# Which engine issues the up matrices: from SP's queue to ScalarE's in a 32-expert loop

## The chip, the cores and the metric

One Trainium2 chip, one core. The metric is the device time of one execution in microseconds (us).

## What is computed

One step of a diffusion backbone for 128 context and 512 latent tokens of width 1024, in fp32: a modulated norm, an input projection, two groups of attention heads (retention and gated linear attention), an output projection, then a mixture of 32 experts. Only the last part touches the change. Every token picks one of 4 groups and in it 2 of 8 experts, and the picked experts are summed with their weights:

```python
def hier_moe(t, ...):
    ...
    for e in range(N_EXPERTS):
        hdn = jax.nn.silu(t @ expert_w_gate[e]) * (t @ expert_w_up[e])
        y = y + combine[:, e:e + 1] * (hdn @ expert_w_down[e]).astype(jnp.float32)
    return y.astype(t.dtype)
```

An expert has three matrices of 1 MB each: gate and up (1024 x 256) and down (256 x 1024). All 32 are used, 96 MB in all, and none of it is used twice.

## The kernel before

Each engine runs a program of its own; semaphores connect them. Up to the router the kernel streams the projection weights through four buffers and builds the attention. The last third of the time is the expert loop.

**Buffers.** There are `WEIGHTS = 7` expert buffers (`exb`, line 36 and below). Each has a gate part, an up part and a down part. The first seven experts are loaded by SP early, as the memory under their buffers comes free (lines 560 to 580). Expert `e` of 7 to 31 goes to buffer `e % 7` and can be loaded only when expert `e - 7` has been used: gate and up when its gate-up product is done (semaphore `gate_up_filled`, in the code `gu_filled`), down when its down product is done (`y_filled`).

**SP** issues the 25 x 3 loads in one order (lines 582 to 587): wait for `gu_filled`, gate (line 524), up (line 525), wait for `y_filled`, down (line 528). A load that is ready stands behind every wait ahead of it. After the last expert SP issues the loads of five blocks of rows (`x_rows`) and of the final norm's row.

**TensorE** runs, for each expert `e`: `gate_up(e + 1)` (line 1850: 32 products of 128x64 against 128x256, which wait for both matrices to land and for the turned tokens), `turn_tokens(e + 2)` (line 1841), `down(e)` (line 1866) and `turn_hidden(e + 1)` (line 1858).

**ScalarE** runs, for each expert: `silu(e + 1)` (line 992) as soon as `gate_up(e + 1)` is done, then `turned_tokens(e + 2)` (line 986), the copy of the turned tokens out of PSUM that `gate_up(e + 2)` waits for. It has a DMA queue of its own, on which it issues `hn_rows` and `x_rows` (lines 969 and 970) before the loop and nothing in the loop.

**VectorE** multiplies silu and up, copies the turned hidden rows and scales the result. **GpSimd** gathers the tokens of the expert four ahead (line 735) and scatters the result rows of each expert (line 744) by indirect DMAs on a third queue.

Of the kernel before, what the change touches and what calls it, by code (L numbers as in the profile page):

```python
# [5 lines left out]
P = 128  # L6
# [12 lines left out]
NE = 32  # L19
# [10 lines left out]
UNIT = KC * ITEM  # L30
# [5 lines left out]
WEIGHTS = 7  # L36
# [143 lines left out]
def build(nc, inp, outs):  # L180
# [10 lines left out]
    with ExitStack() as ctx:  # L191
# [3 lines left out]
        def sem(name):  # L195
            return ctx.enter_context(nc.semaphore(name))
# [116 lines left out]
        exb = [A[:, n * 3 * UNIT:(n + 1) * 3 * UNIT] for n in range(3)] + [B[:, n * 3 * UNIT:(n + 1) * 3 * UNIT] for n in range(3)]  # L313
# [47 lines left out]
        def where(job):  # L361
            n = job_at[job]
            return n % NB1, n // NB1
# [4 lines left out]
        def is_filled(eng, job):  # L368
            b, turn = where(job)
            eng.wait_ge(filled[b], turn + 1)  # L370
# [31 lines left out]
        for i in range(len(IN_ITEMS)):  # L402
            n = i - LEVEL_AFTER + 1
# [22 lines left out]
        for job, block in plan_outputs():  # L426
            n = BLOCKS_OUT.index(block) if block else None
# [28 lines left out]
        def w_src(n):  # L456

            load, slot = LOADS[n], ring[n % RING]
            if load[0] == "ada":
                _, m, i = load  # L460
                return (w_ada[0].rearrange("(p k) c -> p k c", k=KC)[:, 2 * i:2 * i + 2, m * D:(m + 1) * D],
                        slot.rearrange("p (k c) -> p k c", k=2))
            if load[0] == "rest":
                c0 = 2 * D + load[1] * ITEM
                return (w_ada[0, :, c0:c0 + ITEM].rearrange("(p k) c -> p k c", k=KC), slot.rearrange("p (k c) -> p k c", k=KC))
            if load[0] == "in":
                _, c0, w = IN_ITEMS[load[1]]
                return (w_in[0, :, c0:c0 + w].rearrange("(k p) c -> p k c", k=KC),
                        slot[:, 0:KC * w].rearrange("p (k c) -> p k c", k=KC))
            return (w_out[0, :, load[1] * ITEM:(load[1] + 1) * ITEM].rearrange("(k p) c -> p k c", k=KC),  # L470
                    slot.rearrange("p (k c) -> p k c", k=KC))

        def load_used(eng, n):

            load = LOADS[n]
            if load[0] == "ada":
                _, m, i = load
                if i < 3:
                    eng.wait_ge(ada_used, 3 * m + i + 1)
                else:  # L480
                    eng.wait_ge(filled[where(("mr",))[0]] if m == 0 else scale_summed, 1)
            elif load[0] == "rest":
                dve.wait(eng, ("acc", load[1]))
            elif load[0] == "in":
                name, _, w = IN_ITEMS[load[1]]
                is_filled(eng, ("v", load[1], CTX) if name in ("gv", "rv") else ("p", load[1], max(1, w // P) - 1, "ctx"))
            else:
                is_filled(eng, ("mix", CTX, load[1]))
# [5 lines left out]
        gu_landed = [sem(f"gate_up_weights{n}_landed") for n in range(WEIGHTS)]  # L494
# [14 lines left out]
        yo_ready, yo_written, over_read = sem("final_ready"), sem("final_written"), sem("overflow_read")  # L509
        factors_ready, factors_begun = sem("row_factors_ready"), sem("row_factors_begun")  # L510

        block = ctx.enter_context(nc.Block())


        @block.sync
        def _(sp):
# [6 lines left out]
            def load_gate_up(e, b, s):  # L523
                sp.dma_start(exb[b][:, 0:UNIT], ewg_v[bass.ds(e * P, P), :]).then_inc(s, 16)  # L524
                sp.dma_start(exb[b][:, UNIT:2 * UNIT], ewu_v[bass.ds(e * P, P), :]).then_inc(s, 16)  # L525

            def load_down(e, b, s):
                sp.dma_start(exd[b], ewd_v[bass.ds(e, 1)].rearrange("e (j p) n -> p (e j) n", p=P)).then_inc(s, 16)  # L528

            ewg_v = ewg.rearrange("a e (p k) f -> (a e p) (k f)", p=P)  # L530
            ewu_v = ewu.rearrange("a e (p k) f -> (a e p) (k f)", p=P)
            ewd_v = ewd.rearrange("a e f n -> (a e) f n")

            def mod_rows(m, dst):
                for cond in range(2):
# [25 lines left out]
            for e in range(3):  # L561
                load_gate_up(e, e, gu_landed[e])
                load_down(e, e, dn_landed[e])
# [5 lines left out]
            load_used(sp, len(LOADS) - 1)  # L569
            load_gate_up(3, 3, gu_landed[3])  # L570
            load_down(3, 3, dn_landed[3])
            dve.wait(sp, ("hn", LT - 1))
            sp.wait_ge(x2_written, 16 * LT)
            load_gate_up(4, 4, gu_landed[4])
            load_down(4, 4, dn_landed[4])
            dve.wait(sp, ("hn", CTX))
            sp.wait_ge(x2_written_ctx, 16)
# [4 lines left out]
            for e in range(WEIGHTS, NE):  # L582
                b = e % WEIGHTS
                sp.wait_ge(gu_filled, e - WEIGHTS + 1)
                load_gate_up(e, b, gu_landed[b])
                sp.wait_ge(y_filled, e - WEIGHTS + 1)
                load_down(e, b, dn_landed[b])
            sp.wait_ge(y_filled, NE - WEIGHTS + 1)
# [6 lines left out]
            with sp.If(n_over > 0):  # L595
                with sp.Fori(0, n_over) as i:
                    e = sp.value_load(over[0:1, bass.ds(i + 1, 1)], min_val=0, max_val=NE - 1)
# [183 lines left out]
        def _(sc):  # L781
# [7 lines left out]
            f = nc.scalar.activation  # L789
# [59 lines left out]
            for i, (name, _, w) in enumerate(IN_ITEMS):  # L849
# [7 lines left out]
                else:  # L857
                    for c in range(max(1, w // P)):
                        n = 2 * (i - 3) + c
                        for part, lo, hi in (("lat", 0, N_LAT), ("ctx", N_LAT, T)):  # L860
# [9 lines left out]
                            elif name in ("rq", "rk"):  # L870
                                a, h = ("rq", "rk").index(name), 2 * ((i - 3) % 2) + c
                                s = float(P) ** -0.5 if a else 1.0
# [32 lines left out]
                n = i - LEVEL_AFTER + 1  # L905
# [75 lines left out]
            def turned_tokens(e, n, free):  # L981

                sc.wait_ge(xg_turned, e + 1)
                if free is not None:
                    sc.wait_ge(gu_filled, free)
                f(xte[n], bank[n][:, :].rearrange("p (k s) -> p k s", k=KC), ACT.Copy).then_inc(xte_ready, 1)

            def silu(e, n, free):
                sc.wait_ge(gu_filled, e + 1)
                if free is not None:  # L990
                    sc.wait_ge(hid_ready, free)
                f(sil[n], bank[2 + n][:, 0:P], ACT.Silu).then_inc(sil_ready, 1)  # L992

            is_filled(sc, ("idx",))
            sc.wait_ge(none_set, 1)
            for e in range(TOKS):
# [3 lines left out]
            turned_tokens(0, 0, None)  # L1000
            dve.wait(sc, "dest")
            silu(0, 0, None)
            turned_tokens(1, 1, None)
            for e in range(NE - 1):
                silu(e + 1, (e + 1) % 2, e if e else None)
                if e + 2 < NE:
                    turned_tokens(e + 2, e % 2, e + 1)
            n_over = sc.value_load(over[0:1, 0:1], min_val=0, max_val=MAX_OVER)
# [967 lines left out]
```

## Time and profile before

| | |
|---|---|
| three runs | 832.07, 832.17, 835.92 us; median 832.17 |
| the profiled execution | 833.67 us, of which the profile's span is 831.9 us |
| TensorE busy | 725.4 us (87% of the span) |
| VectorE, ScalarE, GpSimd busy | 393.4, 155.7, 206.9 us |
| moved by DMA | 186.02 MB, mean 224 GB/s over the span |
| SP's queue | 159.94 MB, ScalarE's 12.55 MB, GpSimd's 12.83 MB |
| first gate-up product of the loop | 547.3 us from the span's start |

A busy share is of one engine. The DMA share is the mean over the core's 16 DMA engines, and can come out a little over 1 because packets overlap. A DMA-issuing instruction is no busy time of its engine: the profile shows how long the engine's sequencer stood in it. How long the data then takes to arrive is told apart, as the time to landing. Windows are counted from the span's start.

### The profile page before, as it was taken

The numbers are of one execution on the slowest core, as the hardware profiler recorded it, in microseconds if no ns is written. First come the engines' busy times: TensorE is split into PE (matmuls) and PEld (weight loads), VectorE is DVE, ScalarE is ACT, GpSimd is POOL, SyncE is SP. The second block draws the span as 40 slices with busy tenths as digits, with TensorE's granted clock in tenths as the row PEclk, the third lists the DMA queues.
The fourth block names the chain that finished last, engine by engine and source line by source line (L and its number), as shares of the span: only waits on it lengthen the run. The fifth ranks groups of instructions, "written<-read, shape, count | busy, mean of one in ns | idle before, by whom it ended". The sixth has DMA issues, their size and how long they took to land.

```text
span 831.9 us, 10844 instructions
## 1 busy us (share of the span) xinstructions
PE 725.4 (87%) x4297; PEld 467.4 (56%) x4297; DVE 393.4 (47%) x782; ACT 155.7 (19%) x257; POOL 206.9 (25%) x239
## 2 busy tenths in 40 slices
PE   3899996999999999999899999889999777788730
PEld 1655553558888565677788885455554433344310
DVE  0462399587576675656734335712233112111227
ACT  2320421011322215313101111111111001001002
POOL 1500044233333101112300000124444323323213
PEclk8989898999999999999999999999999999989975
DMA  9945304322233434335249317949999999999955
GB/s 353 369 146 155 102 1 137 117 82 94 79 102 102 131 123 137 103 118 144 71 180 404 155 51 299 369 143 368 374 380 384 397 387 389 394 390 385 386 199 240
DMA packets 74307, 186.02 MB, mean 224 GB/s; under 512 B 10012, under 2 KB 47044, under 8 KB 65296
## 3 DMA queue, kind: packets, MB, share of 16 engines
q1 hardware_dynamic: 62688, 159.94, 52.3%
q0 software_dynamic: 6144, 12.83, 4.7%
q10 hardware_dynamic: 5424, 12.55, 4.0%
q8 instruction: 35, 0.57, 0.3%
q14 instruction: 16, 0.13, 0.0%
HBM read 174.48 MB, written 17.10 MB: 230 GB/s over the span
## 4 chain that ended last, share of the span: by engine, by line
PE 61%; DMA 12%; DVE 11%; SPq 8%; issue 3%; ACT 2%; POOL 2%; DVEq 0%; POOLq 0%; ACTq 0%
PE bank L1633 18%; DMA weights_x_h<-in_expert_w_up 10%; PE bank L1850 7%; PE bank L1796 7%; PE bank L1623 4%; PE bank L1866 4%; SPq L525 3%; DVE qkv_gates_tables L1113 3%; SPq L524 3%; SPq L528 2%; DMA weights_x_h<-in_w_ada 2%; PE bank L1661 2%; PE bank L1752 2%; PE bank L1743 2%; PE bank L1695 2%
## 5 line engine op out<-in xcount | busy, mean ns | idle before, releaser
L1633 PE MATMUL bank<-weights_x_h 128*128 128x128 f32 (+3 forms) x672 | 190.7, 445 | 1.4 <-DVE weights_x_h L1079 1.4
L1633 PEld LDWEIGHTS bank<-weights_x_h 128*128 128x128 f32 (+1 forms) x672 | 103.5, 191 | 89.6 <-issue 88.2
L1850 PE MATMUL bank<-qkv_gates_tables,attention 128*64 128x256 f32 x480 | 59.4, 403 | 16.5 <-DMA qkv_gates_tables<-in_expert_w_up 15.6
L1448 DVE TENSOR_TENSOR attention<-attention,bank 128x128 f32<-128x128 f32 x32 | 9.2, 288 | 135.8 <-ACT attention L992 135.8
L1623 PE MATMUL bank<-weights_x_h 128*128 128x256 f32 x320 | 70.3, 380 | 0.0
L1623 PEld LDWEIGHTS bank<-weights_x_h 128*128 128x128 f32 x320 | 60.4, 190 | 9.3 <-DVE attention L1097 0.8
L1850 PE MATMUL bank<-weights_x_h,attention 128*64 128x256 f32 x416 | 52.2, 408 | 13.6 <-DMA weights_x_h<-in_expert_w_up 13.6
L1796 PE MATMUL bank<-weights_x_h 128*128 128x256 f32 x256 | 57.8, 388 | 0.0
L1850 PEld LDWEIGHTS bank<-qkv_gates_tables,attention 128*64 128x64 f32 x480 | 35.6, 146 | 35.9 <-DMA qkv_gates_tables<-in_expert_w_up 17.2
L635 POOL TENSOR_TENSOR small<-small 128x1 f32<-128x1 f32 (+1 forms) x20 | 15.7, 783 | 153.9 <-DVE small L1033 153.9
L1796 PEld LDWEIGHTS bank<-weights_x_h 128*128 128x128 f32 x256 | 49.6, 195 | 7.0
L1469 DVE SCALAR_TENSOR_TENSOR attention<-bank,slot_weights,qkv_gates_tables 128x512 f32<-128x512 f32 x32 | 24.0, 751 | 61.7 <-PE bank L1866 61.7
L1113 DVE SCALAR_TENSOR_TENSOR qkv_gates_tables<-weights_x_h,small,qkv_gates_tables 128x256 f32<-128x256 f32 x112 | 51.1, 536 | 0.0
L1850 PEld LDWEIGHTS bank<-weights_x_h,attention 128*64 128x64 f32 x416 | 30.8, 146 | 31.2 <-DMA weights_x_h<-in_expert_w_up 14.9
L1113 DVE SCALAR_TENSOR_TENSOR weights_x_h<-weights_x_h,small 128x256 f32<-128x256 f32 x112 | 48.0, 506 | 0.0
L992 ACT ACTIVATE attention<-bank 128x128 f32<-128x128 f32 x32 | 8.9, 278 | 203.5 <-PE bank L1850 203.4
L684 POOL TENSOR_TENSOR qkv_gates_tables<-qkv_gates_tables 128x512 f32<-128x512 f32 x8 | 15.2, 1895 | 114.4 <-ACT qkv_gates_tables L880 114.4
L744 POOL DMA_INDIRECT pick_rows<-attention,slot_rows_now x32 | 32.5, 1016 | 28.1 <-POOL slot_rows_now L741 28.1
L735 POOL DMA_INDIRECT attention<-hn_rows,slot_tokens_now x32 | 31.4, 982 | 28.0 <-POOL slot_tokens_now L730 24.6
L741 POOL COPY slot_rows_now<-slot_rows 128x1 int32<-128x1 int32 x32 | 22.6, 707 | 43.4 <-DVE attention L1469 43.4
L730 POOL COPY slot_tokens_now<-slot_tokens 64x1 int32<-64x1 int32 x32 | 5.8, 180 | 102.6 <-PE bank L1841 75.0
L1866 PE MATMUL bank<-qkv_gates_tables,attention 128*64 128x512 f32 x120 | 29.0, 604 | 0.0
(286 smaller groups left out, 997.9 us busy)
## 6 DMA issues: line engine op xcount, KB each, us to landing
weights_x_h<-in_w_ada SPq DMA_DIRECT2D x24, 1024.0 KB, 7.7
qkv_gates_tables<-in_expert_w_gate SPq DMA_DIRECT2D x15, 1024.0 KB, 19.0
qkv_gates_tables<-in_expert_w_up SPq DMA_DIRECT2D x15, 1024.0 KB, 27.2
qkv_gates_tables<-in_expert_w_down SPq DMA_DIRECT2D x15, 1024.0 KB, 26.7
weights_x_h<-in_w_in SPq DMA_DIRECT2D x14, 1024.0 KB, 7.6
weights_x_h<-in_expert_w_gate SPq DMA_DIRECT2D x13, 1024.0 KB, 20.9
weights_x_h<-in_expert_w_up SPq DMA_DIRECT2D x13, 1024.0 KB, 26.4
weights_x_h<-in_expert_w_down SPq DMA_DIRECT2D x13, 1024.0 KB, 26.6
```

Of the source, the lines that this page charges most:

```text
L524: sp.dma_start(exb[b][:, 0:UNIT], ewg_v[bass.ds(e * P, P), :]).then_inc(s, 16)
L525: sp.dma_start(exb[b][:, UNIT:2 * UNIT], ewu_v[bass.ds(e * P, P), :]).then_inc(s, 16)
L735: pool.indirect_dma_start(xg[b], None, hn_dram[:, :], bass.IndirectOffsetOnAxis(ap=idxc[b][:, :].bitcast(U32), axis=0), bounds_check=T - 1 ...
L741: nc.gpsimd.tensor_copy(sidxc[n][:, :], sidx[:, col]).then_inc(sidxc_set, 1)
L744: pool.indirect_dma_start(ys_dram[:, :], bass.IndirectOffsetOnAxis(ap=sidxc[n][:, :].bitcast(U32), axis=0), yb[n], None, bounds_check=2 * ...
L1113: ins = v.scalar_tensor_tensor(acc, w[:, k], cS[:, a, k:k + 1], acc, ALU.mult, ALU.add)
L1469: v.scalar_tensor_tensor(yb[n], bank[4 + n][:, :], weight, g2s[n], ALU.mult, ALU.mult).then_inc(y_ready, 1)
L1623: ins = mm(ps[:, 0:ITEM], hT[:, k, t * P:(t + 1) * P], wt[:, k, :], start=(k == 0), stop=(k == KC - 1))
L1633: ins = mm(ps[0:m, 0:hi - lo], wt[:, k, c * m:(c + 1) * m], hT[:, k, lo:hi], start=(k == 0), stop=(k == KC - 1))
L1796: ins = mm(ps[:, 0:ITEM], hT[:, k, t * P:(t + 1) * P], wt[:, k, :], start=(k == 0), stop=(k == KC - 1))
L1850: ins = mm(bank[2 + n][j * SLOTS:(j + 1) * SLOTS, 0:2 * P], xte[n][:, k, :], exgu[b][:, :, k, j * P:(j + 1) * P], start=(k == 0), stop=(k ...
L1866: ins = mm(bank[4 + n][half * SLOTS:(half + 1) * SLOTS, :], hidT[n][:, j, :], exd[b][:, j, half * 512:(half + 1) * 512], start=(j == 0), s ...
```

## The change

The up matrices of experts 7 to 31 are issued by ScalarE on its own queue, each behind the silu of the expert that used the buffer before. SP issues gate and down as before. The loads of experts 0 to 6 and those of the overflow loop keep their place. The three views of the weights move out of SP's block so that both can use them.

```diff
+            def load_gate(e, b, s):
+                sp.dma_start(exb[b][:, 0:UNIT], ewg_v[bass.ds(e * P, P), :]).then_inc(s, 16)
...
             for e in range(WEIGHTS, NE):
                 b = e % WEIGHTS
                 sp.wait_ge(gu_filled, e - WEIGHTS + 1)
-                load_gate_up(e, b, gu_landed[b])
+                load_gate(e, b, gu_landed[b])
                 sp.wait_ge(y_filled, e - WEIGHTS + 1)
                 load_down(e, b, dn_landed[b])
...
+            def load_up(e, b, s):
+                sc.dma_start(exb[b][:, UNIT:2 * UNIT], ewu_v[e * P:(e + 1) * P, :]).then_inc(s, 16)
...
             silu(0, 0, None)
+            load_up(WEIGHTS, 0, gu_landed[0])
             turned_tokens(1, 1, None)
             for e in range(NE - 1):
                 silu(e + 1, (e + 1) % 2, e if e else None)
+                if e + 1 + WEIGHTS < NE:
+                    load_up(e + 1 + WEIGHTS, (e + 1) % WEIGHTS, gu_landed[(e + 1) % WEIGHTS])
                 if e + 2 < NE:
                     turned_tokens(e + 2, e % 2, e + 1)
```

ScalarE in the loop, before (L992 is the silu, L986 the copy of the turned tokens; `attention` is the memory area that holds both results):

```order
L992 ACTIVATE attention<-bank3 128x128
L986 ACTIVATE attention<-bank0 128x512
L992 ACTIVATE attention<-bank2 128x128
L986 ACTIVATE attention<-bank1 128x512
L992 ACTIVATE attention<-bank3 128x128
```

and with the change, at the experts whose buffers lie in the areas `attention` and `qkv_gates_tables` (L995 is the silu, L998 the new issue, L989 the copy):

```order
L995 ACTIVATE attention<-bank2 128x128
L998 DMA attention<-in_expert_w_up 128x2048
L989 ACTIVATE attention<-bank1 128x512
L995 ACTIVATE attention<-bank3 128x128
L998 DMA qkv_gates_tables<-in_expert_w_up 128x2048
L989 ACTIVATE attention<-bank0 128x512
```

The issue stands between the silu and the copy that TensorE's next gate-up product waits for.

SP's queue from expert 7 on, before:

```order
L524 DMA qkv_gates_tables<-in_expert_w_gate 128x2048
L525 DMA qkv_gates_tables<-in_expert_w_up 128x2048
L528 DMA qkv_gates_tables<-in_expert_w_down 128x2x1024
L524 DMA qkv_gates_tables<-in_expert_w_gate 128x2048
L525 DMA qkv_gates_tables<-in_expert_w_up 128x2048
```

and with the change (L532 gate, L535 down), each with the semaphore that it waits for:

```order
L532 DMA qkv_gates_tables<-in_expert_w_gate 128x2048 [waits gate_up_filled]
L535 DMA qkv_gates_tables<-in_expert_w_down 128x2x1024 [waits expert_done]
L532 DMA qkv_gates_tables<-in_expert_w_gate 128x2048 [waits gate_up_filled]
L535 DMA qkv_gates_tables<-in_expert_w_down 128x2x1024 [waits expert_done]
L532 DMA weights_x_h<-in_expert_w_gate 128x2048 [waits gate_up_filled]
```

The up matrix has left the queue; before, it stood behind the wait for the down product (`expert_done`) of the expert before its own.

## Rows read from the trace of the kernel before

**Rows 1.** The page: the span in 40 slices, busy tenths of the DMA engines.

```profile
DMA  9945304322233434335249317949999999999955
```

**Rows 2.** Windows of the expert loop; columns as in the first line.

```profile
core 0: us, PE busy (x) PEld busy (x) DVE busy (x) ACT busy (x) POOL busy (x), PEclk, DMA share, GB/s
...
553.00:557.00 4.00, 3.95 (x34) 2.43 (x35) 0.95 (x2) 0.07 (x1) 0.62 (x1) 1.00 1.00 421
558.00:559.00 1.00, 1.00 (x8) 0.29 (x4) 0.00 (x0) 0.26 (x1) 0.28 (x1) 1.00 0.42 103
559.00:560.00 1.00, 1.00 (x9) 0.39 (x7) 0.38 (x1) 0.00 (x0) 0.68 (x1) 1.00 0.09 16
560.00:561.00 1.00, 1.00 (x12) 0.68 (x10) 1.00 (x3) 0.00 (x0) 0.46 (x1) 1.00 0.65 94
561.00:562.00 1.00, 1.00 (x12) 0.68 (x10) 0.23 (x1) 0.00 (x0) 0.27 (x1) 1.00 0.66 238
...
570.00:633.00 63.00, 63.00 (x486) 33.84 (x486) 18.95 (x40) 8.53 (x20) 28.71 (x40) 1.00 1.02 375
633.00:785.00 152.00, 119.81 (x837) 62.58 (x835) 32.23 (x68) 14.87 (x34) 47.16 (x65) 0.92 1.02 391
```

**Rows 3.** Timeline of SP's queue: start us, us, engine line op out<-in.

```profile
550.96 0.33 SPq L524 DMA_DIRECT2D qkv_gates_tables<-in_expert_w_gate  x1
...
559.53 0.38 SPq L528 DMA_DIRECT2D qkv_gates_tables<-in_expert_w_down  x1
...
561.29 0.94 SPq L525 DMA_DIRECT2D qkv_gates_tables<-in_expert_w_up  x1
...
600.30 7.87 SPq L525 DMA_DIRECT2D qkv_gates_tables<-in_expert_w_up  x1
```

**Rows 4.** Timeline of TensorE and ScalarE at experts 0 to 2.

```profile
552.30 0.28 ACT L992 ACTIVATE attention<-bank 128x128 f32<-128x128 f32 x1
...
553.31 3.67 PE L1850 MATMUL bank<-qkv_gates_tables,attention 128*64 128x256 f32 x32
...
557.03 0.28 ACT L992 ACTIVATE attention<-bank 128x128 f32<-128x128 f32 x1 [3.97 <-PE bank L1850]
...
557.66 0.60 ACT L986 ACTIVATE attention<-bank 128x512 f32<-128x512 f32 x1 [0.35 <-PE bank L1841]
...
559.68 3.67 PE L1850 MATMUL bank<-qkv_gates_tables,attention 128*64 128x256 f32 x32
```

**Rows 5.** Timeline of TensorE: gate-up products of experts 15 and 31.

```profile
644.27 3.67 PE L1850 MATMUL bank<-qkv_gates_tables,attention 128*64 128x256 f32 x32 [1.67 <-DMA qkv_gates_tables<-in_expert_w_up]
...
789.59 3.67 PE L1850 MATMUL bank<-weights_x_h,attention 128*64 128x256 f32 x32 [1.30 <-DMA weights_x_h<-in_expert_w_up]
```

**Rows 6.** Line 525 on SP's queue: ns min/median/max, first and last start us.

```profile
L525 SPq DMA_DIRECT2D qkv_gates_tables<-in_expert_w_up x15: 432/2613/7865, 432.0 to 752.8; - x15
```

**Rows 7.** Timeline of ScalarE's and SP's queues near 442 us.

```profile
441.80 0.33 ACTq L969 DMA_DIRECT2D hn_rows<-attention  x1
442.17 0.45 ACTq L970 DMA_DIRECT2D x_rows<-weights_x_h  x1
...
441.31 1.24 SPq L566 DMA_DIRECT2D onorm<-mod_rows  x1
442.58 4.08 SPq L566 DMA_DIRECT2D onorm<-mod_rows  x1
```

**Rows 8.** DMA issues: out<-in, queue, count, KB each, median us to landing.

```profile
hn_rows<-attention ACTq DMA_DIRECT2D x5, 512.0 KB, 6.8
...
onorm<-mod_rows SPq DMA_DIRECT2D x4, 128.0 KB, 21.9
```

**Rows 9.** Windows before the loop, columns as in rows 2.

```profile
515.00:520.00 5.00, 5.00 (x13) 2.15 (x12) 4.38 (x27) 0.00 (x0) 0.00 (x0) 1.00 1.00 411
440.00:445.00 5.00, 5.00 (x25) 4.41 (x24) 2.44 (x3) 0.00 (x0) 0.00 (x0) 1.00 1.04 398
445.00:450.00 5.00, 4.36 (x25) 3.66 (x23) 1.87 (x3) 1.04 (x2) 0.00 (x0) 1.00 0.97 375
```

More of the change, by code:

```diff
@@ L510, in build @@
         factors_ready, factors_begun = sem("row_factors_ready"), sem("row_factors_begun")
+        ewg_v = ewg.rearrange("a e (p k) f -> (a e p) (k f)", p=P)
+        ewu_v = ewu.rearrange("a e (p k) f -> (a e p) (k f)", p=P)
+        ewd_v = ewd.rearrange("a e f n -> (a e) f n")
         block = ctx.enter_context(nc.Block())
@@ L525, in load_gate_up @@
                 sp.dma_start(exb[b][:, UNIT:2 * UNIT], ewu_v[bass.ds(e * P, P), :]).then_inc(s, 16)
+            def load_gate(e, b, s):
+                sp.dma_start(exb[b][:, 0:UNIT], ewg_v[bass.ds(e * P, P), :]).then_inc(s, 16)
             def load_down(e, b, s):
                 sp.dma_start(exd[b], ewd_v[bass.ds(e, 1)].rearrange("e (j p) n -> p (e j) n", p=P)).then_inc(s, 16)
-            ewg_v = ewg.rearrange("a e (p k) f -> (a e p) (k f)", p=P)
-            ewu_v = ewu.rearrange("a e (p k) f -> (a e p) (k f)", p=P)
-            ewd_v = ewd.rearrange("a e f n -> (a e) f n")
             def mod_rows(m, dst):
```

## The prediction

> **What bounds the kernel now.** I read three views, in this order. First the page's row of DMA activity [rows 1]: from the slice that begins near 562 us to the one that ends near 790 us the sixteen DMA engines stand at 9 tenths or more, which they do nowhere else for long. So the expert loop is where the change can matter, and the transfers are the first suspect. Second the windows of that stretch [rows 2]: the DMA share is 1.02 from 570 to 785 us, at 375 and then 391 GB/s, so no engine has idle time there; only between 558 and 562 us is there a hole, with shares of 0.42, 0.09, 0.65 and 0.66. Third, TensorE's own rows. While it still lives on the seven buffered experts it starts a gate-up product every 559.68 - 553.31 = 6.37 us [rows 4]; later it starts one every (789.59 - 644.27) / 16 = 9.08 us and waits each time for an up matrix to land [rows 5]. 9.08 is more than 6.37, so from about expert 15 the transfers alone set the pace, and they have been behind since 562 us. What SP does follows from that: its issues, 0.33 us when nothing is queued, grow to 2.61 us in the median and 7.87 us at most [rows 3, 6], because the queue in front of it is full. That time on SP looks like a bound and is none: the engines behind it are at 1.02 all the while.
>
> **The change, part by part.** Transfers, bytes and destinations stay the same; 25 up matrices (experts 7 to 31) change issuer and place in the order.
>
> *Removed from SP:* 25 issues, 2.61 us each in the median [rows 6], some 65 us of SP's time. They cost nothing now and give nothing back: while SP stands in them, the engines are full [rows 2]. The cover is the backlog of matrices that are issued and not yet moved; if it were gone, an issue would be back at 0.33 us anyway. The Trainium skill says the same in general (DMA: Bandwidth & Descriptors, section Issuing engines are not separate DMA queues): starting transfers from several engines saves only the time of initiating them, since all run on the same engines. By that rule alone the change would give 832.2, the upper end of the forecast's own range below; the rows go beyond it in one place, the hole, because an issue there is late and not long.
>
> *The hole, the one gain.* SP waits in order: gate and up of expert 7 at 550.96 us, then a wait until `down(0)` is done, at 559.53, for down 7, then gate 8, and up 8 only at 561.29 [rows 3]. But the buffer of up 8 is free when the gate-up product of expert 1 ends, and ScalarE knows this: its silu of expert 1 runs from 557.03 to 557.31 [rows 4]. With the change up 8 is issued at 557.31, 4 us earlier than now and 2.2 us before anything else. Gate 7 shows how long an issue takes to reach the engines: issued at 550.96, they are full by 553 [rows 2, 3], so up to 2.0 us. Up 8 then runs from about 559, for 1.05 MB / 421 GB/s = 2.5 us, until down 7 and gate 8 arrive after 561.5 as now. It fills the idle shares of 559 to 562: 0.91 + 0.35 + 0.34 = 1.60 us of all engines. Below that the gain could be 0, if the engine that ends last was not one of the idle ones; above it 2.18 us, the whole hole from 558 on. I take 1.6, since a share of 0.09 means that nearly every engine stood still. All that follows is transfer-bound, so a head start of 1.6 us stays a head start until the last gate lands.
>
> *Up 7* is now issued behind the first silu, whose end is 552.30 + 0.28 = 552.58 [rows 4], about 1.3 us later than its present place right behind gate 7. Gate 7 occupies the engines until about 553 + 2.5 = 555.5, so up 7 still finds them busy: nothing.
>
> *Added to ScalarE:* 25 issues at 0.33 to 0.45 us [rows 7], 11 us in all, between a silu and the copy of the next but one expert's turned tokens. That copy now starts at 557.66, 0.35 us behind the silu's end, and ends at 558.26; TensorE needs it at 559.68 [rows 4], 1.42 us later. An issue of 0.45 us moves it by 0.1 us: nothing. Behind the copy nothing is queued on ScalarE but the next silu, which waits for the next gate-up product.
>
> *Order of the transfers.* Ups no longer stand behind gates and downs. What is issued on ScalarE's queue lands sooner than what was issued on SP's at the same time: 512 KB of `hn_rows` took 6.8 us in the median, the 128 KB of `onorm` on SP's full queue 21.9 us [rows 8]. So ups will land several experts ahead, and TensorE will wait for gates. Up to the last seven experts that changes nothing, as the total number of bytes sets the pace: the last gate lands when all but the last down and the final rows have been moved, just as the last up does now. TensorE then needs the same steps to the end as behind 789.59 now.
>
> *Sum.* The profiled execution took 833.67 us, with a span of 831.9; minus 1.6 that is 832.07. The three runs have their median at 832.17, 1.50 below the profiled one, so the forecast is 832.17 - 1.6, about **830.5 us**. Its own range, from a gain of 2.2 to none, is 830.0 to 832.2.
>
> **The rivals.**
>
> *A, faster: two queues move more than one.* From 570 to 633 us the engines are full but move 375 GB/s, against 411 where the same matrices run without the tokens' gathers and scatters [rows 2, 9]. If each engine could go on with a second queue while the first stalls, at most all of this would come back: 223 us from 562 to 785 at 386, the weighted mean of the two long windows, would shrink by 223 x (1 - 386/411) = 13.6 us, to 817; half of it to 824. Against it: the stretches with both queues in use, 440 to 450 us, show 398 and 375 GB/s, not more than 411 [rows 9].
>
> *B, slower: ScalarE is held in its issue as SP is.* If an issue on ScalarE had to wait until SP's current one is through, its length X would be SP's 2.61 plus half of another, 3.9 us. The copy of the tokens would then end at 557.31 + X + 0.60, past the 559.68 at which TensorE needs it from X = 1.77 us on, and the step per expert would be 6.37 + X - 1.77 = 4.60 + X. 24 such steps and six of 6.37 take as long as today's 553.31 to 789.59, less 1.6, at X = 3.6 us: from there on it decides. At 3.9 they take 242.2 against 236.3 us, so the time is 832.2 + 5.9 = 838. Against it: at 441.80 and 442.17 us ScalarE issued twice while SP was inside issues of 1.24 and 4.08 us (441.31 and 442.58), and needed 0.33 and 0.45 us, no more than otherwise [rows 7]. The Trainium skill speaks for this rival (Perfetto Trace Analysis, section DMA Instruction — HWDGE (DVE, Sync)): the generator of descriptors is locked by one issuer until it has written them all. The two ScalarE rows do not agree with a lock that lasts as long as SP's issues, but they are only two.
>
> *C, the head start is given back at the end.* If ups land seven experts ahead, the last seven bring only gate and down: 9.08 x 2/3 = 6.05 us of transfers against 6.37 us of TensorE. TensorE falls behind by up to 7 x 0.32 = 2.2 us, and the time is 832.7. For it: the landings of [rows 8]. Against it: the share of tokens' traffic in 9.08 does not shrink by a third, so 6.05 is a lower bound.
>
> *D, slower: two queues move less.* The two windows of [rows 9] with both in use have a mean of 386 GB/s against 411, 6% less. Were that the cost of mixing, it would hold for as long as ups and others run together, two thirds of 223 us: 8.9 us, so 832.2 - 1.6 + 8.9 = 839.5. Against it: those stretches also write rows to memory, which the loop's ups do not.
>
> **How the numbers follow.** Forecast 0.56, A 0.16, B 0.08, C 0.14, D 0.06. Half a percent, 4.2 us, is about what a measurement of this kernel can tell from no change. Forecast and C lie within it, 0.70; A is faster, 0.16; B and D are slower, 0.14. The range takes in forecast, C and the smaller half of A and of D's price: 825.5 to 836.0; left out are the larger half of A, 0.08, B, 0.08, and a part of D, 0.04.
>
> **What would show it.** In the changed profile the up issues stand on ScalarE's queue at 0.33 to 0.5 us each, the first near 552.6 and the second near 557.3; the DMA share between 559 and 562 us is near 1; TensorE's waits name a gate in place of an up; its pace in the transfer-bound part is 9 us per expert in the mean, though with ups far ahead the waits may be uneven; the last gate-up product starts 1 to 2 us before 789.59. Ups landing about 5 to 10 us after their issue would confirm the order. The forecast is wrong if the GB/s between 570 and 785 us move by more than 2% either way (A or D), if ScalarE's issues are longer than 2 us in the median (B), or if the transfer-bound stretch is followed by experts that start every 6.4 us without a wait (C).

## The result, and the profile after

The changed kernel takes **839.04 us** in the median of 20 runs (834.47 to 841.39), the kernel before on the same chip 834.44 (20 runs, 831.6 to 836.6): a ratio of **1.0053**, 95% interval 1.0039 to 1.0067, so +4.4 us (3.3 to 5.6). The forecast was 830.5, in a range that ended at 836.0. The profiled execution took 837.82 us (span 836.1) against 833.67: +4.15. Of these, 793.60 - 789.59 = 4.0 stand between the starts of the last gate-up product, after a loop that began only 0.6 us later (547.85 against 547.25).

In the changed kernel the gate is issued in L532, the down in L535, the up on ScalarE's queue in L998; silu is L995, the gate-up product L1859.

The page, DMA digits and queues (packets, MB, share):

```profile
DMA  9945304322233434235339318859999999999945
...
q1 hardware_dynamic: 59088, 133.73, 43.8%
q10 hardware_dynamic: 9024, 38.77, 12.6%
```

26.2 MB moved from SP's queue (q1) to ScalarE's (q10), as the change says. Windows of the changed kernel, with the columns of [rows 2]:

```profile
558.00:559.00 1.00, 1.00 (x8) 0.42 (x8) 0.23 (x1) 0.60 (x1) 0.18 (x1) 1.00 0.97 246
559.00:560.00 1.00, 1.00 (x6) 0.14 (x2) 0.00 (x0) 0.00 (x0) 0.69 (x1) 1.00 1.02 258
560.00:561.00 1.00, 1.00 (x11) 0.65 (x11) 0.79 (x2) 0.00 (x0) 0.28 (x1) 1.00 0.98 393
561.00:562.00 1.00, 1.00 (x12) 0.70 (x10) 0.82 (x2) 0.00 (x0) 0.73 (x1) 1.00 0.95 389
...
562.00:633.00 71.00, 64.86 (x490) 34.52 (x486) 18.75 (x40) 8.74 (x20) 28.84 (x40) 0.95 1.02 368
633.00:740.00 107.00, 82.11 (x562) 43.09 (x559) 21.06 (x45) 9.62 (x22) 33.24 (x46) 0.87 1.02 386
740.00:780.00 40.00, 36.02 (x262) 18.85 (x261) 9.77 (x21) 5.25 (x12) 14.54 (x20) 0.96 1.02 377
```

And the last three windows of the kernel before, cut in the same way:

```profile
562.00:633.00 71.00, 71.00 (x551) 38.22 (x549) 20.84 (x44) 9.62 (x22) 32.66 (x45) 1.00 1.02 377
633.00:740.00 107.00, 81.83 (x578) 42.60 (x576) 22.75 (x48) 10.50 (x24) 35.03 (x49) 0.93 1.02 388
740.00:780.00 40.00, 33.17 (x228) 17.45 (x226) 7.87 (x17) 4.21 (x10) 10.42 (x14) 0.88 1.02 400
```

Three things are to be seen. The hole of [rows 2] is gone: 0.95 to 1.02 where 0.42, 0.09, 0.65 and 0.66 stood. The engines are as full as before from 562 us on (1.02), but carry less: 368 against 377 GB/s up to 633 us, 386 against 388 from there to 740, and 377 against 400 from 740 to 780. A full DMA share is no measure of the rate. And TensorE is busier from 740 to 780 us, 36.02 against 33.17 us, so it has less idle time and more left to do.

The lower rate up to 633 us is in the packets themselves. The queues from 562 to 633 us (packets, MB, share of the 16 engines), first in the kernel before, then in the changed kernel:

```profile
q1 hardware_dynamic: 4092, 22.81, 85.8%
```

```profile
q1 hardware_dynamic: 2548, 12.74, 49.1%
q10 hardware_dynamic: 1326, 9.59, 37.1%
```

Before, 0.858 x 16 x 71 us of engine time for 22.81 MB is 42.7 us of one engine for each MB. In the changed kernel it is 43.8 on SP's queue and 43.9 on ScalarE's.

TensorE's last gate-up products, in its timeline of the changed kernel (start us, us; in brackets the idle time before, and what ended it):

```profile
751.85 5.36 PE L1859 MATMUL bank<-weights_x_h,attention 128*64 128x256 f32 x32 [2.70 <-DMA weights_x_h<-in_expert_w_gate]
...
761.25 3.67 PE L1859 MATMUL bank<-weights_x_h,attention 128*64 128x256 f32 x32 [1.28 <-DMA weights_x_h<-in_expert_w_gate]
...
767.68 3.67 PE L1859 MATMUL bank<-attention 128*64 128x256 f32 x32
...
774.05 3.67 PE L1859 MATMUL bank<-qkv_gates_tables,attention 128*64 128x256 f32 x32
...
780.86 3.67 PE L1859 MATMUL bank<-qkv_gates_tables,attention 128*64 128x256 f32 x32 [0.37 <-DMA qkv_gates_tables<-in_expert_w_gate]
...
787.23 3.67 PE L1859 MATMUL bank<-qkv_gates_tables,attention 128*64 128x256 f32 x32
...
793.60 3.67 PE L1859 MATMUL bank<-weights_x_h,attention 128*64 128x256 f32 x32
```

The last six stand 6.4 to 6.8 us apart, with one wait of 0.37 us: TensorE's own pace, as on the buffered experts of [rows 4], while the kernel before still waited for an up ahead of the last one [rows 5]. In the 4 us ahead of the last product the transfers are already running out, more so than before; first the changed kernel's window, then the one before:

```profile
789.60:793.60 4.00, 4.00 (x31) 1.78 (x25) 0.37 (x2) 0.88 (x2) 0.98 (x1) 1.00 0.65 262
```

```profile
785.60:789.60 4.00, 2.70 (x19) 1.06 (x18) 1.75 (x4) 0.84 (x2) 0.55 (x1) 1.00 0.86 338
```

The table of waits of the changed kernel (line waited for: us in all, times, longest us) names gates:

```profile
PE bank L1859 <- DMA qkv_gates_tables<-in_expert_w_gate: 16.1, 5, 6.5
PE bank L1859 <- DMA weights_x_h<-in_expert_w_gate: 16.0, 4, 6.1
...
PE bank L1859 <- DMA attention<-in_expert_w_gate: 3.3, 1, 3.3
```

10 waits with 35.4 us, where the kernel before had 17 for ups with 33.5, none over 3.3: as much waiting, in fewer and longer pieces. ScalarE's and SP's queues in the changed kernel's timeline (start us, us the issuer stood in it):

```profile
557.63 0.28 ACT L995 ACTIVATE attention<-bank 128x128 f32<-128x128 f32 x1 [3.97 <-PE bank L1859]
557.63 0.34 ACTq L998 DMA_DIRECT2D qkv_gates_tables<-in_expert_w_up  x1
...
601.89 20.45 SPq L532 DMA_DIRECT2D qkv_gates_tables<-in_expert_w_gate  x1
...
602.25 0.33 ACTq L998 DMA_DIRECT2D qkv_gates_tables<-in_expert_w_up  x1
...
608.62 0.33 ACTq L998 DMA_DIRECT2D qkv_gates_tables<-in_expert_w_up  x1
...
614.99 0.34 ACTq L998 DMA_DIRECT2D weights_x_h<-in_expert_w_up  x1
```

While SP stood 20.45 us in one issue, ScalarE made three, each in 0.33 us.

### The profile page after: what moved, and what is told of

Read it like the earlier page. It is cut to its first block, busy times and chain, and to the rows that moved or that the text cites. A ratio compares the mean times of both kernels' runs of the same rounds, so it can differ in the third digit from the quotient of the medians.

```text
span 836.1 us, 10844 instructions
## 1 busy us (share of the span) xinstructions
PE 727.1 (87%) x4297; PEld 468.5 (56%) x4297; DVE 393.5 (47%) x782; ACT 156.0 (19%) x257; POOL 207.9 (25%) x239
## 3 DMA queue, kind: packets, MB, share of 16 engines
q1 hardware_dynamic: 59088, 133.73, 43.8%
q0 software_dynamic: 6144, 12.83, 4.6%
## 4 chain that ended last, share of the span: by engine, by line
PE 56%; DMA 26%; DVE 11%; issue 3%; ACT 2%; POOL 2%; SPq 0%; DVEq 0%; POOLq 0%; ACTq 0%
PE bank L1642 18%; DMA qkv_gates_tables<-in_expert_w_gate 13%; DMA weights_x_h<-in_expert_w_gate 10%; PE bank L1805 7%; PE bank L1859 5%; PE bank L1632 4%; DVE qkv_gates_tables L1122 3%; DMA weights_x_h<-in_w_ada 2%; PE bank L1761 2%; PE bank L1670 2%; PE bank L1875 2%; PE bank L1752 2%; PE bank L1704 2%; PE bank L1582 1%; PE bank L1548 1%
## 5 line engine op out<-in xcount | busy, mean ns | idle before, releaser
L1859 PE MATMUL bank<-qkv_gates_tables,attention 128*64 128x256 f32 x480 | 59.5, 404 | 17.0 <-DMA qkv_gates_tables<-in_expert_w_gate 16.1
L1859 PE MATMUL bank<-weights_x_h,attention 128*64 128x256 f32 x416 | 52.9, 412 | 16.0 <-DMA weights_x_h<-in_expert_w_gate 16.0
L1859 PEld LDWEIGHTS bank<-qkv_gates_tables,attention 128*64 128x64 f32 x480 | 35.6, 145 | 36.1 <-DMA qkv_gates_tables<-in_expert_w_gate 17.0
L1859 PEld LDWEIGHTS bank<-weights_x_h,attention 128*64 128x64 f32 x416 | 31.2, 148 | 33.6 <-DMA weights_x_h<-in_expert_w_gate 16.7
L995 ACT ACTIVATE attention<-bank 128x128 f32<-128x128 f32 x32 | 8.9, 278 | 206.9 <-PE bank L1859 196.6
```

The lines of the kernel that those rows point to most:

```text
L1859: ins = mm(bank[2 + n][j * SLOTS:(j + 1) * SLOTS, 0:2 * P], xte[n][:, k, :], exgu[b][:, :, k, j * P:(j + 1) * P], start=(k == 0), stop=(k ...
```

## The experiments

Two theories stood at the start. **R (rate):** two hardware queues with a backlog each move less. **T (tail):** the ups have run ahead, the last experts bring only gate and down, and TensorE becomes the bound there. All differences below are the ratio to the kernel before, run beside it on the same chip, times 834.4 us, with the 95% interval.

### e1_first_three, e2_first_half, e6_second_half: only some ups on ScalarE's queue

The ups of experts 7 to 9 (e1), 7 to 18 (e2), or 19 to 31 (e6) go over ScalarE, the others over SP as before. The diff is that of e1; e2 has 19 for 10, and e6 the condition turned round at 19, without the first load of ScalarE:

```diff
-                load_gate(e, b, gu_landed[b])
+                (load_gate if e < 10 else load_gate_up)(e, b, gu_landed[b])
...
-                if e + 1 + WEIGHTS < NE:
+                if e + 1 + WEIGHTS < 10:
```

> Only the up matrices of experts 7 to 9 are issued by ScalarE, those of 10 to 31 by SP as before. Theory T (order): ups on a queue of their own land several experts ahead of their gates, the last experts then need only gates and downs, and TensorE at 6.4 us per expert sets the end. Theory R (rate): two queues beside the tokens' gathers and scatters move fewer bytes per us. Either way only the filled hole between 558 and 562 us is left here, 1.6 us: ratio to before 0.998. If the hole is worth nothing, 1.000. The DMA share between 559 and 562 us is near 1.

> Up matrices of experts 7 to 18 by ScalarE, of 19 to 31 by SP as before. After the change the time was 4.6 us above before, so with the hole's 1.6 us there are 6.2 us of loss to explain. T: nothing is ahead at the end, no loss, ratio 0.998. R: the two queues run together for about half of the loop, half of the loss, 3.1 - 1.6 = +1.5 us, ratio 1.002. The last gate-up products start 8 to 9.5 us apart and not 6.4 in either theory.

> The complement: ups of experts 7 to 18 by SP as before, of 19 to 31 by ScalarE. The hole stays open. T: the ups are ahead at the end, full loss without the gain, +6.2 us, ratio 1.007. R: half of the loss, +3.1 us, ratio 1.004.

Measured: e1 832.89 us, 0.998 (0.9967 to 0.9994), -1.7 us; e2 834.3, 1.0003 (0.999 to 1.0017), +0.3; e6 838.21, 1.0046 (1.0031 to 1.006), +3.8. So the hole is worth about the 1.6 us of the forecast (0.5 to 2.8); nine more ups of the first half cost 0.3 + 1.7 = 2.0; the second half costs 3.8 (2.6 to 5.0). Their sum, 4.1, is the changed kernel's 4.4 within the intervals. One expectation was missed: the last two products of e2 start 6.37 us apart (783.78 and 790.15), not 8 to 9.5, and so do those of e1 (780.77 and 787.14), so one such pair is no tail yet. The windows of e2, then those of e6, then that of e7 (below), which uses SP's queue alone:

```profile
562.00:633.00 71.00, 67.15 (x496) 35.73 (x494) 18.95 (x40) 8.74 (x20) 29.55 (x41) 0.95 1.02 370
```

```profile
562.00:633.00 71.00, 71.00 (x553) 38.23 (x549) 21.07 (x45) 9.89 (x23) 32.03 (x45) 1.00 1.02 377
...
633.00:740.00 107.00, 74.48 (x504) 38.54 (x505) 20.60 (x44) 9.34 (x21) 30.86 (x43) 0.87 1.02 390
```

```profile
562.00:633.00 71.00, 71.00 (x551) 38.22 (x549) 20.84 (x44) 9.62 (x22) 32.25 (x45) 1.00 1.02 373
```

The two halves lose in different ways. From 562 to 633 us the five kernels whose ups run on ScalarE's queue beside a backlog of gates and downs move 368 to 372 GB/s (the changed kernel and e4 368, e2 and e8 370, e3 372); the six that have SP's queue alone there, or nearly so, move 373 to 377 (e7 373, e11 374, e5 375, e1 376, the kernel before and e6 377). The groups do not overlap, but each figure is of one execution and they lie close, so the fall is 1 to 2% and its size is loose. More gathers are not the reason: 10 are issued in that stretch in the changed kernel, 11 before. In e6, with its ups in the second half, the rate from 633 to 740 us is not lower (390 against 388), although they run beside a backlog there too; but its last six products start 6.37 us apart, the last at 793.76, as in the changed kernel, and in the 4 us ahead of the last one its engines are down to a share of 0.37.

### e3_three_ahead: all ups on ScalarE's queue, but three experts ahead instead of seven

```diff
-                if e + 1 + WEIGHTS < NE:
-                    load_up(e + 1 + WEIGHTS, (e + 1) % WEIGHTS, gu_landed[(e + 1) % WEIGHTS])
+                n = e + 1 + WEIGHTS if e < 2 else e + 1 + 3
+                if n < NE and (e < 2 or n >= 10):
+                    load_up(n, n % WEIGHTS, gu_landed[n % WEIGHTS])
```

> All ups 7 to 31 on ScalarE's queue, 7 to 9 as in the change, but from expert 10 on each is issued only three experts before it is used. T: ups are ahead by at most three experts instead of seven, the loss is 3/7 of 6.2 = 2.7 us, less 1.6 = +1.1 us, ratio 1.001. R: the queues run together as before, loss unchanged, +4.6 us, ratio 1.0055.

Measured: 837.54 us, 1.0037 (1.0022 to 1.0053), +3.1 us. The timeline of TensorE shows no tail; it waits for ups up to expert 30:

```profile
784.00 5.36 PE L1860 MATMUL bank<-qkv_gates_tables,attention 128*64 128x256 f32 x32 [1.92 <-DMA qkv_gates_tables<-in_expert_w_up]
...
792.06 3.67 PE L1860 MATMUL bank<-weights_x_h,attention 128*64 128x256 f32 x32
```

So T alone is not the cause. Its windows show where mixing costs: nothing while ScalarE issues no up (after up 9 at 561.34 us the next, up 10, follows at 593.21), then 364 GB/s from 600 to 633 us, where the six kernels on SP's queue alone, or nearly so, move 375 to 380 (windows this short swing: e7, on SP's queue, shows 367 and 379 in these two):

```profile
562.00:600.00 38.00, 38.00 (x294) 20.34 (x292) 11.19 (x24) 5.21 (x12) 17.40 (x24) 1.00 1.02 379
600.00:633.00 33.00, 33.00 (x254) 17.59 (x254) 9.64 (x21) 4.97 (x11) 14.66 (x21) 1.00 1.02 364
```

### e4_after_short_tail, e5_before_short_tail: TensorE's work cut at the end

The gate-up products of experts 26 to 30 are made shorter, in the changed kernel (e4) and in the kernel before (e5):

```diff
-                for k in range(KC):
+                for k in range(KC // 2 if 26 <= e <= 30 else KC):
```

> The changed kernel, with half of the gate-up product left out for experts 26 to 30 (its sum runs over half of the rows), so TensorE needs some 1.8 us less for each of these five. T: TensorE no longer sets the pace at the end, the whole loss of 6.2 us goes or what of it is tail: up to -6 us against the change, ratio to before 0.998. R: the transfers set the end, unchanged against the change, ratio 1.0055.

> The kernel before, with the same half of the gate-up product left out for experts 26 to 30. The control for the run above: in both theories the transfers set the end here, ratio to before 1.000.

Measured: e4 835.97 us, 1.0022 (1.0008 to 1.0036), 2.6 us less than the changed kernel's ratio. The control e5 did not stay where it was: 836.27, 1.0016 (1.0006 to 1.0027), +1.3 us, and one profile of it shows what fits. From the first gate-up product to the last it takes as long as the kernel before (787.16 - 544.91 = 242.25 against 789.59 - 547.25 = 242.34 us), but the last product itself takes 5.36 us in place of 3.67:

```profile
787.16 5.36 PE L1850 MATMUL bank<-weights_x_h,attention 128*64 128x256 f32 x32 [3.31 <-DMA weights_x_h<-in_expert_w_up]
```

TensorE, with less to do, had waited 3.31 us ahead of it, and its granted clock from 789 to 791 us is 0.50 (the lower level, 1.2 GHz). In the profile of e4 the last product ran at a granted clock of 1.00 in 3.67 us, so nothing of the control's loss has to be added there: the tail is worth 2.6 us, with about 1.7 to either side. In e4 the last product waits for its gate again. It starts 790.20 - 546.03 = 244.17 us after the first one, in the changed kernel 793.60 - 547.85 = 245.75:

```profile
790.20 3.67 PE L1859 MATMUL bank<-weights_x_h,attention 128*64 128x256 f32 x32 [0.22 <-DMA weights_x_h<-in_expert_w_gate]
```

### e8_landings: how far the ups run ahead

```diff
+        up_landed = [sem(f"up_weights{n}_landed") for n in range(WEIGHTS)]
...
-                    te.wait_ge(gu_landed[n % WEIGHTS], 32 * (n // WEIGHTS + 1))
+                    te.wait_ge(gu_landed[n % WEIGHTS], 32 + 16 * (n // WEIGHTS))
+                    if n >= WEIGHTS:
+                        te.wait_ge(up_landed[n % WEIGHTS], 16 * (n // WEIGHTS))
```

> The changed kernel with one thing more: the up matrices of experts 7 to 31 have landing semaphores of their own, so that the trace shows the landing of each matrix. Nothing else is changed, so the time should be the changed kernel's, 839 +- 1 us, if the theory holds that TensorE waited for gates because of their landing and not because both matrices share a semaphore. Order theory (ups run ahead): ups land 8 to 15 us after their issue in ScalarE's queue, gates and downs 25 to 35 us after theirs, and from expert 15 on every up has landed at least 20 us before TensorE uses it. If ups instead land 20 us or more after their issue, the two queues share the engines evenly and the tail theory (the last experts bring only gate and down) loses its ground.

Measured: 838.89 us, 1.0068 (1.0045 to 1.009), the changed kernel's time. Its DMA issues (queue, count, KB each, median us to landing over those that the trace resolves):

```profile
weights_x_h<-in_expert_w_gate SPq DMA_DIRECT2D x13, 1024.0 KB, 37.0
...
qkv_gates_tables<-in_expert_w_up ACTq DMA_DIRECT2D x12, 1024.0 KB
weights_x_h<-in_expert_w_up ACTq DMA_DIRECT2D x10, 1024.0 KB, 11.7
...
attention<-in_expert_w_up ACTq DMA_DIRECT2D x3, 1024.0 KB, 10.9
```

An up lands 11 us after its issue, within the 8 to 15 expected; a gate lands 37 us after its own, later than the 25 to 35 expected. An up is issued some 40 us or more ahead of its use (7 products at 6.37 us or more, less the one of 3.67 us that it waits for), so it has landed over 20 us ahead, as expected. That ups overtake gates is what the forecast had drawn from [rows 8]. The Trainium skill (DMA: Bandwidth & Descriptors, section Queues, rings and completion order) says that each engine takes turns between the queues for which it has work, a packet at a time; by that rule the short queue overtakes the long one, and the trace agrees (11.7 against 37.0).

### e9_before_one_row, e10_after_one_row, e12_half_one_row: without the gathers

GpSimd's gather of an expert's token rows becomes a plain transfer of one row, in the kernel before (e9), the changed kernel (e10) and e2 (e12); the 32 scatters stay:

```diff
-                pool.indirect_dma_start(xg[b], None, hn_dram[:, :], bass.IndirectOffsetOnAxis(ap=idxc[b][:, :].bitcast(U32), axis=0),
-                                        bounds_check=T - 1, oob_is_err=False).then_inc(xg_landed[b], 16)
+                pool.dma_start(xg[b][0:1, :], hn_dram[0:1, :]).then_inc(xg_landed[b], 16)
```

> Control for the next run: the kernel before, with each expert's gather of token rows cut to a plain transfer of one row (the tokens are then the wrong ones; the 32 scatters stay). It takes 6.4 MB, a half of GpSimd's queue in the loop, off the engines: at 386 GB/s some 16 us, but 7 of the 32 gathers lie before the transfer-bound stretch and the two ends stay, so 8 to 13 us faster, 821 to 826 us. No theory of the change speaks here.

> The changed kernel with the same cut of the gathers. Compare with the control above. Theory G (two hardware queues cost because GpSimd's gathers are a third party in the engines): the loss of 4.6 us falls to 2.5 or less. Theory Q (two hardware queues cost by themselves, and the tail by the order): the difference to the control stays at 3.5 to 6 us. Tail alone: with fewer bytes the engines need less than 9.08 us for an expert and less than 6.37 for its gate and down, so TensorE paces earlier, the tail grows, and the difference is over 6 us.

> The kernel of e2 (ups of experts 7 to 18 on ScalarE's queue, 19 to 31 on SP's) with the gathers cut to one row as in e9 and e10 (wrong tokens). Without the gathers the windows of e10 and e9 moved the same 417 to 419 GB/s, and between 550 and 570 us e10 moved 38 x 12 + 58 x 8 = 0.92 MB more, 2.2 us at 417 GB/s; yet it took 1.2 us more than e9. If the mixing is free without gathers and e10's loss is all in the last experts (tail theory), this kernel has the gain of the hole alone: 2.2 us under e9's 805.3, so 803.1, ratio 0.962 to 0.965, 570 to 740 us at 417 GB/s or more, and its last two gate-up products start over 7 us apart. If the mixing itself costs also without gathers, it comes to 805 to 806.5, ratio 0.966 to 0.9675.

Measured: e9 805.33 us, 0.966 (0.9636 to 0.9683); e10 806.5, 0.9674 (0.9656 to 0.9692); e12 801.15, 0.9618 (0.9597 to 0.9639). The control itself was a miss: 28 us faster, not 8 to 13. The windows of e9, e10 and e12 in turn say why:

```profile
600.00:633.00 33.00, 33.00 (x256) 17.82 (x258) 10.55 (x23) 4.37 (x10) 12.52 (x21) 1.00 1.02 417
633.00:740.00 107.00, 97.24 (x750) 52.01 (x747) 28.97 (x61) 13.12 (x30) 38.73 (x62) 1.00 1.02 417
```

```profile
562.00:600.00 38.00, 38.00 (x294) 20.42 (x294) 11.20 (x24) 5.25 (x12) 14.96 (x24) 1.00 1.02 415
600.00:633.00 33.00, 33.00 (x256) 17.85 (x258) 10.56 (x23) 4.37 (x10) 12.53 (x21) 1.00 1.02 419
633.00:740.00 107.00, 90.86 (x698) 48.41 (x696) 27.06 (x57) 12.24 (x28) 35.21 (x57) 1.00 1.02 417
```

```profile
562.00:600.00 38.00, 38.00 (x296) 20.36 (x292) 11.37 (x24) 5.25 (x12) 14.84 (x25) 1.00 1.02 418
```

The gathers cost more than their bytes: without them everything moves at 417 GB/s in place of 377 to 388. And without them two hardware queues move what one does, 415 to 419. e10 is 0.9674 - 0.9660 = 0.14% or 1.2 us slower than e9, within the 2.5 that theory G allowed. So G holds for the rate: its fall needs the gathers as a third party. e12, which mixes in the first half and has no tail, is 0.9660 - 0.9618 = 0.42% or 3.5 us faster than e9. That is about the hole, which is larger in e9 than in the kernel before: a share of 0.23 from 557 to 562 us against 0.60 (e12 0.92, 3.5 us of all engines more than e9). e10 differs from e12 by the second half alone and is 0.56% or 4.7 us slower: that is the tail, without any loss of rate. Not all of the 4.7 need be tail: in the profiled execution of e10 (and in those of e8 and e9) the second gate-up product took 5.36 us in place of 3.67, at a granted clock of 0.50 (1.2 GHz) from 555 to 558 us, after the same work as in the changed kernel, which kept 1.00 there. The last products of e10 and e12, from TensorE's timelines:

```profile
757.18 3.67 PE L1858 MATMUL bank<-qkv_gates_tables,attention 128*64 128x256 f32 x32
...
763.55 3.68 PE L1858 MATMUL bank<-weights_x_h,attention 128*64 128x256 f32 x32
```

```profile
740.11 3.67 PE L1858 MATMUL bank<-qkv_gates_tables,attention 128*64 128x256 f32 x32 [1.36 <-DMA qkv_gates_tables<-in_expert_w_up]
...
748.43 5.36 PE L1858 MATMUL bank<-qkv_gates_tables,attention 128*64 128x256 f32 x32 [1.88 <-DMA qkv_gates_tables<-in_expert_w_up]
...
756.53 3.67 PE L1858 MATMUL bank<-weights_x_h,attention 128*64 128x256 f32 x32
```

6.37 us apart without a wait in e10, over 8 us in e12, whose engines stand at 1.02 in the 4 us ahead of the last product (e10 0.87). Each of these differences is between ratios whose intervals are 0.2% wide to either side, so the sizes are good to 2 us or so; the windows carry the verdict on the rate.

### e7_sp_reordered, e11_sp_reordered_first: the hole filled on SP's own queue

SP issues gate and up of the next expert before it waits for this expert's down buffer, for all experts (e7) or up to expert 12 (e11). ScalarE issues nothing:

```diff
-                sp.wait_ge(gu_filled, e - WEIGHTS + 1)
-                load_gate_up(e, b, gu_landed[b])
+                if e == WEIGHTS:
+                    sp.wait_ge(gu_filled, 1)
+                    load_gate_up(e, b, gu_landed[b])
+                if e + 1 < NE:
+                    sp.wait_ge(gu_filled, e - WEIGHTS + 2)
+                    load_gate_up(e + 1, (e + 1) % WEIGHTS, gu_landed[(e + 1) % WEIGHTS])
                 sp.wait_ge(y_filled, e - WEIGHTS + 1)
                 load_down(e, b, dn_landed[b])
```

> No second queue: SP issues gate and up of expert e+1 before it waits for the buffer of down e, in the order in which TensorE uses them. Both theories: the hole is filled (gate and up 8 are issued near 557 us instead of 560 to 561), nothing else changes, ratio 0.998, -1.6 us. If the hole is worth nothing, 1.000.

> SP's queue alone, with the order of e7 (gate and up of the next expert before the wait for this expert's down) only up to expert 12, and the old order from there on. If e7's 3.8 us are the hole (1.7) and the new order at the end (2.1), this run shows only the first: 832.0 to 833.5 us, a ratio of 0.997 to 0.999. If the whole 3.8 come from the hole, it comes to 830.9 like e7; if from the order at the end alone, to 834.4.

Measured: e7 **830.86 us**, 0.9954 (0.9936 to 0.9972), -3.8 us, faster than both kernels; e11 831.42, 0.9976 (0.9963 to 0.9988), -2.0 us, the hole again. The last product of e7 still waits for an up, and starts 3.8 us earlier than the 789.59 of [rows 5]:

```profile
785.78 3.67 PE L1854 MATMUL bank<-weights_x_h,attention 128*64 128x256 f32 x32 [1.34 <-DMA weights_x_h<-in_expert_w_up]
```

The remaining 1.8 us (the two intervals just overlap) fit the new order of e7 behind expert 12: gate 31, up 31, down 30, down 31, the order in which TensorE uses them. The traces show that this lead does not arise at the end alone. Counted from the first gate-up product, e7 starts that of expert 16 at 101.98 us and e11 at 104.65, and that of expert 31 at 238.03 and 240.49. About 2.5 us is also the time of the one down matrix that each gate and up overtake (1.05 MB at 389 GB/s: 2.7 us). Behind the last product e7 gives 1.0 us back (43.3 us to the end of its span, 42.3 in e11).

## Why the prediction was wrong

*The hole: right.* Priced at 1.6 us; the engines are full where they stood idle, and e1 and e11 put it at 1.7 and 2.0, each with 1.1 us to either side.

*SP's issues and ScalarE's issues at nothing: right.* SP now stands up to 20.45 us in one issue and TensorE's waits are as long as before; ScalarE's stay at 0.33 to 0.35 us. Rival B falls with that. The three issues inside SP's one don't agree with the lock of which the Trainium skill tells (Perfetto Trace Analysis, section DMA Instruction — HWDGE (DVE, Sync)). A small point was off: an up is issued when silu starts, not behind its end (557.63 for both), as the issue does not wait for the activation that it follows in the program.

*Order of the transfers: the step that failed.* The forecast had the mechanism (ups land experts ahead, TensorE waits for gates) and said: "Up to the last seven experts that changes nothing, as the total number of bytes sets the pace". Bytes set the pace only at a given rate, and the rate was not given. The forecast had taken the share of 1.02 for it. Where ups and SP's backlog ran together, up to 633 us, the same full share carried 368 in place of 377 GB/s: 71 us x 9 GB/s = 0.64 MB, 1.7 us, which e2 less e1 puts at 2.0. That is rival D, with 2.4% for 71 us where D had priced 6% for two thirds of the loop. Against D the prediction had only that the stretches of [rows 9] also write rows to memory, which the loop's ups do not. It did not ask what the loop has in place of those: GpSimd's gathers, without which, by e9, e10 and e12, two queues move as much as one.

*And the end, the other half of that step.* The forecast took the last seven experts as transfer-bound too ("TensorE then needs the same steps to the end as behind 789.59 now"). That is rival C, priced at up to 2.2 us with the remark that 6.05 us for gate and down is a lower bound. TensorE did become the bound: 6.4 to 6.8 us per expert for the last six, with the engines at 0.65 in the 4 us ahead of the last product. e6 has the cost at 3.8 us, e4 against the changed kernel at 2.6, and e10 against e12 at up to 4.7 with faster transfers. The sum of hole, rate and end is -1.7 + 2.0 + 3.8 = +4.1 with e6's price and +2.9 with e4's; the measured 4.4 (3.3 to 5.6) is nearer the first, and no run settles the size closer than that. Of the prediction's own signs, that of C came (experts every 6.4 us without a wait behind the transfer-bound stretch); that of D, a change of over 2% between 570 and 785 us, just did not (380 against 386 GB/s, 1.6%).

*C and D were treated as alternatives.* Both happened at once, and each could be read from [rows 8]: ups that overtake mean that two queues are drawn from together (D) and that there is nothing left of them at the end (C). The forecast accepted the overtaking and let its consequences stand as rivals with 0.14 and 0.06.

*By the Trainium skill's rule* that starting transfers from several engines saves only the time of initiating (DMA: Bandwidth & Descriptors, section Issuing engines are not separate DMA queues) the time would have been 832.2. The measured 839.04 does not agree: a second queue also changes the order and, beside the gathers, the rate.

Open: the mixing costs rate up to 633 us, but from 633 to 740 us the changed kernel shows 386 against 388 GB/s and e6 390, and no run tells why. The gathers stand closer in the first stretch, 11 in 71 us before against 12 in the 107 us behind it, which would fit theory G and was not tested. In e3 all of the loss is in the transfers, yet only part of its 4.8 us (3.1 and the hole) is in the windows shown. How the gathers slow the other queues was not tried, beyond taking them away.

## What to carry to other kernels

In a transfer-bound stretch a second queue made no bandwidth here (415 to 419 GB/s with two queues, 417 with one); it changes the order of landing, and what was pulled ahead is missing at the end, where another engine may then become the bound. Put transfers in the order of use, and fill a hole in the queue that has it by moving a wait, before spreading the load over queues: e7's few lines gained 3.8 us where the second queue lost 4.4. Judge a stretch by GB/s beside the DMA share, since 368, 377 and 417 GB/s all stood at the same full share of 1.02.

## What the runs showed that I had not expected

- Indirect gathers slow everything that shares the engines. The 32 gathers, 12.83 - 7.71 = 5.1 MB on GpSimd's queue by the pages of the kernel before and e9, would be 12.3 us at 417 GB/s; without them the kernel is 28 us faster, and the long stretch moves 417 in place of 377 to 388 GB/s at the same share of 1.02.
- An issue on ScalarE's queue goes out at the instant at which the activation ahead of it starts (557.63 us for both).
- Less work on TensorE at the end made the kernel before slower (e5, +1.3 us, 0.5 to 2.3). In its profile the last product ran in 5.36 us in place of 3.67, at a granted clock of 0.50 from 789 to 791 us, after a wait of 3.31 us.
